# The residual's transposes for the next stage, issued in parts ahead of and between the last products of the sum that completes it, at five places

## What is computed

```
for l in range(2):
    h = rmsnorm(x, g_mix[l]);  z = h @ w_in[l]
    ... short convolution and forgetting attention on z ...
    x = x + concat([y_conv, y_fox]) @ w_out[l]
    hx = rmsnorm(x, g_xa[l])
    x = x + mem_cross_attention(hx, ...) @ w_xo[l]
    hf = rmsnorm(x, g_ffn[l])
    x = x + (swiglu(hf, ...) if l == 0 else moe_swiglu(hf, ...))
```

## Time and profile before

| what | us |
|---|---|
| median of 3 runs | 1334.91 |
| lowest and highest run | 1333.96, 1335.45 |
| span of the profiled execution | 1334.4 |
| PE busy in it | 1313.6 (98%) |
| DVE busy | 1013.7 (76%) |
| ACT busy | 833.1 (62%) |
| POOL busy | 84.6 (6%) |

### The profile page before, as it was taken

One profiled execution on the slowest core, in us unless ns is written; L12 is line 12 of the kernel. 1 busy time (PEld: TensorE's weight loads), 2 busy tenths in 40 slices (PEclk: granted clock), 3 DMA queues, 4 the chain that ended last, 5 costly groups with the idle time before them and its releaser, 6 DMA issues.

```text
span 1334.4 us, 17846 instructions
## 1 busy us (share of the span) xinstructions
PE 1313.6 (98%) x6726; PEld 1122.7 (84%) x6726; DVE 1013.7 (76%) x782; ACT 833.1 (62%) x746; POOL 84.6 (6%) x105
## 2 busy tenths in 40 slices
PE   8999999999999999899999999999999999999998
PEld 6998888888889878788888888888888888888886
DVE  5767764444565776688888888888889888888988
ACT  5545554444455545476767777678677667777674
POOL 4201010000012010200000000000000000000000
PEclk9999999999999999899999999999999999999999
DMA  9633436655597335299999999899999998998994
GB/s 323 195 118 122 151 106 195 200 187 186 181 376 270 122 101 193 66 399 376 341 386 384 346 403 386 347 408 354 374 387 351 399 382 340 417 380 341 413 396 177
DMA packets 117035, 386.18 MB, mean 289 GB/s; under 512 B 6289, under 2 KB 33533, under 8 KB 116989
## 3 DMA queue, kind: packets, MB, share of 16 engines
q1 hardware_dynamic: 105068, 365.08, 73.1%
q0 software_dynamic: 3168, 11.54, 2.2%
q10 hardware_dynamic: 8752, 8.92, 1.9%
HBM read 369.79 MB, written 15.73 MB: 289 GB/s over the span
## 4 chain that ended last, share of the span: by engine, by line
PE 83%; DVE 8%; DMA 3%; ACT 2%; issue 2%; POOL 1%; SPq 0%; DVEq 0%; ACTq 0%
PE bank L1688 34%; PE bank L1684 23%; PE bank L1685 23%; DVE wl L1166 2%; DMA ring<-in_we_gate 2%; DVE wl L1180 2%; PE bank L2264 1%; ACT wh L808 1%; DVE scratch L1324 1%; DVE scratch L1302 1%; DMA ring<-in_we_up 1%; DVE aT_low L1185 1%; PE bank L1877 0%; POOL mfox L693 0%; PE bank L1709 0%
## 5 line engine op out<-in xcount | busy, mean ns | idle before, releaser
L1180 DVE TENSOR_TENSOR wl<-ring,wh 128x2816 fp32r<-128x2816 f32 (+1 forms) x127 | 400.2, 3171 | 58.5 <-PE bank L1688 33.6
L808 ACT ACTIVATE wh<-ring 128x2816 fp32r<-128x2816 f32 (+1 forms) x128 | 336.7, 2632 | 148.1 <-DMA ring<-in_we_gate 43.7
L1166 DVE TENSOR_TENSOR wl<-ring,wh 128x2048 fp32r<-128x2048 f32 (+3 forms) x78 | 185.9, 2383 | 117.0 <-ACT wh L794 116.2
L1684 PE MATMUL bank<-wh,xh 128*128 128x512 f32 (+1 forms) x696 | 264.8, 380 | 4.4 <-DVE wl L1180 3.1
L1685 PE MATMUL bank<-wh,xl 128*128 128x512 f32 (+1 forms) x696 | 263.1, 378 | 0.0
L1688 PE MATMUL bank<-wl,xh 128*128 128x512 f32 (+1 forms) x944 | 241.8, 378 | 0.0
L794 ACT ACTIVATE wh<-ring 128x2048 fp32r<-128x2048 f32 (+3 forms) x77 | 152.8, 1984 | 114.1 <-PE bank L1685 101.2
L1180 DVE TENSOR_TENSOR wl<-ring,wh_third 128x2816 fp32r<-128x2816 f32 (+1 forms) x64 | 187.1, 2923 | 26.7 <-PE bank L1688 23.8
L1688 PEld LDWEIGHTS bank<-wl,xh 128*128 128x128 f32 x944 | 174.8, 188 | 25.4
L808 ACT ACTIVATE wh_third<-ring 128x2816 fp32r<-128x2816 f32 (+1 forms) x64 | 155.5, 2430 | 34.6 <-DMA ring<-in_we_up 16.0
L1684 PEld LDWEIGHTS bank<-wh,xh 128*128 128x128 f32 x696 | 130.6, 188 | 31.2 <-issue 5.6
(11 more groups left out here) (266 smaller groups left out, 1584.2 us busy)
## 6 DMA issues: line engine op xcount, KB each, us to landing
ring<-in_we_gate SPq DMA_DIRECT2D x64, 1408.0 KB, 7.9
ring<-in_we_up SPq DMA_DIRECT2D x64, 1408.0 KB, 8.2
ring<-in_we_down SPq DMA_DIRECT2D x56, 1536.0 KB, 8.8
ring<-in_w_in SPq DMA_DIRECT2D x8, 1536.0 KB, 11.7
ring<-in_w_gate SPq DMA_DIRECT2D x10, 1024.0 KB, 5.1
ring<-in_w_up SPq DMA_DIRECT2D x10, 1024.0 KB, 5.1
ring<-in_w_down SPq DMA_DIRECT2D x10, 1024.0 KB, 4.9
ring<-in_w_in SPq DMA_DIRECT2D x9, 1024.0 KB, 8.6
```

Source lines behind the costliest of these rows:

```text
L808: nc.scalar.activation(wh_in_pass(j, n), ring[:, slot, 0:n], ACT.Copy).then_inc(high_ready, 1)
L1166: nc.vector.tensor_tensor(wl[:, j, 0:n], ring[:, slot, 0:n], wh[:, j, 0:n].bitcast(F32), ALU.subtract).then_inc(low_ready, 1)
L1180: nc.vector.tensor_tensor(wl[:, j % 2, 0:n], ring[:, pass_slot(j), 0:n], wh_in_pass(j, n).bitcast(F32), ALU.subtract).then_inc(low_ready, 1)
L1684: nc.tensor.matmul(dst, x_high, w_high, start=first, stop=False)
```

## The change

`residual_transposed` is cut so that a caller names the row block and the quarters. At five places (`yT` and `zT` of both layers, `xT` of layer 1) the 16 transposes are no longer issued in one run behind the last product. Instead, with the last weight tile: all eight of row block 0 ahead of bank 3's high products; the first four of row block 1 (quarters 0 and 1) between bank 3's high and low products; and the last four (quarters 2 and 3) behind bank 3's low products. The waits of each transpose are as before. `xT` of layer 0, whose residual comes from a transfer, keeps its order. ACT gets one added wait in layer 1: for bank `xw3`, ahead of `gained`.

```diff
                 if l > 0:
+                    act.wait_ge(*full(l, "xw3"))
                     gained(l, "zT", "ffn")
...
-            def residual_transposed(l, names, added):
-                for t in range(TT):
...
+            def residual_transposed(l, names, added, t, quarters):
+                if added is None:
+                    pe.wait_ge(x_loaded[t], 16)
+                for i in quarters:
+                    ps = open_bank(l, f"{names}{i}") if t == 0 else bank(l, f"{names}{i}")
+                    if added is not None and i % 2 == 0:
+                        pe.wait_ge(*taken(0 if added == "d" else l, f"{added}{2 * t + i // 2}"))
+                    for k in range(2):
+                        c = (2 * i + k) * P
+                        ins = nc.tensor.transpose(ps[:, k * S + t * P:k * S + t * P + P], xres[:, t, c:c + P], ident[:])
+                    if t == TT - 1:
+                        ins.then_inc(done(l, f"{names}{i}"), 1)
+
+            def first_rows_transposed(l, names, added):
+                residual_transposed(l, names, added, 0, range(4))
+
+            def second_rows_transposed(l, names, added, half):
+                residual_transposed(l, names, added, 1, (2 * half, 2 * half + 1))
...
-                residual_transposed(l, "xT", None if l == 0 else "d")
+                if l == 0:
+                    first_rows_transposed(l, "xT", None)
+                    second_rows_transposed(l, "xT", None, 0)
+                    second_rows_transposed(l, "xT", None, 1)
+                else:
+                    second_rows_transposed(l, "xT", "d", 1)
...
                         for i in range(4):
                             if last:
+                                if i == 3:
+                                    first_rows_transposed(l, next_input, names)
                                 ins = products(i, False)
                                 if i == 3:
                                     ins.then_inc(highs_used, 1)
+                                    second_rows_transposed(l, next_input, names, 0)
...
-                token_projection("wo", "wo", KT, range(2, 4), {j: taken(l, f"oT{j - 2}") for j in (2, 3)})
-
-
-                residual_transposed(l, "yT", "wo")
+                token_projection("wo", "wo", KT, range(2, 4), {j: taken(l, f"oT{j - 2}") for j in (2, 3)},
+                                 next_input="yT")
+
+
+                second_rows_transposed(l, "yT", "wo", 1)
...
-                residual_transposed(l, "zT", "xw")
+                token_projection("xw", "xo", XH, range(2), {j: taken(l, f"xo{j}") for j in range(2)}, last_heads, "zT")
+
+
+                second_rows_transposed(l, "zT", "xw", 1)
...
                         for q in range(4):
+                            if last and q == 3:
+                                first_rows_transposed(1, "xT", "d")
                             ins = products(q, False)
                             if last:
                                 if q == 3:
                                     ins.then_inc(highs_used, 1)
+                                    second_rows_transposed(1, "xT", "d", 0)
                                 products(q, True).then_inc(done(0, f"d{q}"), 1)
```

More of the change, by code:

```diff
@@ L1991, in heads_transposed, with token_projection @@
                         ins.then_inc(done(l, f"oT{i}"), 1)
-                def token_projection(names, fill, rows, ss, waits, inside=None):
+                def token_projection(names, fill, rows, ss, waits, inside=None, next_input=None):
                     for j in ss:
@@ L2096, in last_heads @@
                     memory_heads(1)
-                token_projection("xw", "xo", XH, range(2), {j: taken(l, f"xo{j}") for j in range(2)}, last_heads)
-                residual_transposed(l, "zT", "xw")
+                token_projection("xw", "xo", XH, range(2), {j: taken(l, f"xo{j}") for j in range(2)}, last_heads, "zT")
+                second_rows_transposed(l, "zT", "xw", 1)
                 if l == 0:
```

## The result

| | us |
|---|---|
| changed kernel, median of 21 runs (lowest to highest) | 1335.36 (1333.23 to 1337.46) |
| kernel before, median of 21 runs on the same chips | 1333.50 (1331.88 to 1335.70) |
| ratio, with its 95% interval | 1.0014 (1.0008 to 1.0020) |
| the same ratio in a second series (11 and 20 runs) | 1.0016 (1.0007 to 1.0025) |
| span of the profiled execution after (before: 1334.4) | 1335.1 |

The change makes the kernel slower by 1.9 us, with an interval of 1.1 to 2.7. I had forecast +3.2 us, 1338.1, with a range from 1335.5. The direction is right, the size is not. The 1335.36 lies just under the range's low end, and that is as much the base as the change: the kernel before has a median of 1333.5 over 21 runs, 1.4 us under the 1334.91 of the three that the prediction started from. With the forecast put on 1333.5, the measured time would still lie 1.3 us under it.

The account below looks back on a forecast made before the run. PE was taken to bound the kernel, busy 1313.6 of 1334.4 us. Delays of 0.8 + 0.8 + 0.33 + 0.4 + 0.9 = 3.2 us on the median 1334.9 gave 1338.1, range 1335.5 to 1340.8.

Parts of the forecast that it names:

- What bounds, and that the place must be late: PE, busy 1313.6 of 1334.4 us, sets the end; at each place the last four transposes wait for the uncovered add.
- The sum: All five places together: 0.8 + 0.8 + 0.33 + 0.4 + 0.9 = 3.2 us slower.
- yT 0.8: yT, each layer: DVE's low parts wait for bank 3 and start later, so the next tile begins 0.8 us later.
- zT 0.33: zT of layer 0: first product 0.46 us later, 0.13 saved by earlier casts, net 0.33 later.
- xT 0.4: xT of layer 1: first product 0.51 us later, 0.12 saved by earlier casts, net 0.4 later.
- logits 0.9: zT of layer 1: the add delays DVE's gain on bank 0, so the logits start 0.9 us later.
- the credit for the early casts: zT of layer 0 and xT of layer 1: first eight products run faster with casts ready, saving 0.13 and 0.12 us.
- 2 for the groups: Rival: moved transpose groups wait for DVE or boundaries cost 0.1 each, adding 1 to 3 us; 1340.1 at middle; chance 0.07.
- Moved transposes and boundaries cost nothing: Twelve transposes per place only end the last products 1.31 us later; no waits; boundaries cost nothing, bound 0 to 1.0 in all.
- partly taken up behind the places: Rival: idle PE time behind the places absorbs delay, leaving 1.9 us at the middle, 1336.8; chance 0.22.
- The rival of the early casts: First products of yT, zT, xT: earlier casts save 4.3 us with logits, against add wait w at five places; chance 0.08.
- The rival of the clock: Routing, 560 to 563 us: moved transposes keep the granted clock high, saving 1.5 us, 1336.6; chance 0.08.

Follow-up runs that it names:

- the two short-add kernels: Changed kernel and kernel before, each with the five last adds covering 1 column instead of 512; first logit -0.04 and +0.03 us against the kernel before.
- after_low_free: Changed kernel, but at yT DVE's input_low no longer waits for the last bank ahead of the first quarter; first logit +1.30 us against the kernel before.
- last_place_old: Changed kernel with the old transpose order at zT of layer 1 alone; first logit +1.80 us against the kernel before, logits 3.71 us.

## Why the prediction was right and wrong

*What bounds, and that the place must be late.* Right. The last add loses its cover, the four transposes behind it wait, and no other stage takes up more than 0.1 of the delay. The idle time of "about 1.2 us" is 1.21 to 1.28, the low parts start 1.5 behind the last product where I had 1.6, and the two short-add kernels show that the add is the cause.

*The sum.* This is the step that failed: 3.2 us of terms where 2.67 stood at the first logit. Term by term, forecast and measured: yT 0.8 and 0.59, zT 0.33 and 0.21, xT 0.4 and 0.30, yT 0.8 and 0.68, logits 0.9 and 0.89. Their errors all point the same way, and come from three places.

At yT the first transpose behind the wait was mis-sized. I took the longest of the line, 0.48, and came to 0.85 from its load to DVE's start; after shows 151.25 to 151.95, 0.70. The 0.48 was no transpose behind such a wait. It stands in the kernel's first microseconds, where every transpose takes 0.42 or more and the clock has not yet risen. The first line is of the kernel before, the second of the changed one:

```profile
L1709 PE MATMUL bank<-ident,xres x16: 421/421/477, 4.8 to 8.1; 128*128 128x128 f32 x16
...
L1709 PE MATMUL bank<-ident,xres x4: 272/272/328, 151.3 to 151.6; 128*128 128x128 f32 x4
```

Behind the wait it took 0.33, and the 0.15 between them is that error: I priced the unknown from the row's maximum without asking where the maximum stands.

At zT and xT the credit for the early casts was mis-sized; the 0.48 is no part of those two terms. I priced the first eight products at 8 x 0.226 = 1.81, so 0.13 and 0.12 saved. Here they are in the changed kernel, at zT of layer 0:

```profile
189.61 1.68 PEld L1689 LDWEIGHTS bank<-wh,xh 128*128 128x128 f32 x8
...
191.34 1.79 PEld L1689 LDWEIGHTS bank<-wl,xh 128*128 128x128 f32 x8
```

They took 191.34 - 189.61 = 1.73, and 1.73 again at xT: 0.21 and 0.20 saved. The other 0.05 at zT are its four transposes, 0.39 from the first load to the next product's where I had 0.44.

A last part at yT: the tile was 0.68 late (0.75 in layer 1), but the stage behind only 0.6 (0.68). Before, DVE's product at 160.18 waited about 0.05 for POOL, which ends at 159.37 + 0.70 = 160.07; after, POOL is not late and DVE's own maximum ends last. The first two lines are of the kernel before:

```profile
159.37 0.70 POOL L724 TENSOR_TENSOR xqr<-xqr,neghalf 128x2 f32<-128x2 f32 x1 [25.66 <-DVEq L1396]
...
160.18 0.16 DVE L1404 TENSOR_TENSOR xnm<-xnm,xqr 128x2 f32<-128x2 f32 x1
...
159.33 0.70 POOL L724 TENSOR_TENSOR xqr<-xqr,neghalf 128x2 f32<-128x2 f32 x1 [25.73 <-DVEq L1397]
159.96 0.69 DVE L1402 TENSOR_REDUCE xnm<-bank 128x2 f32<-128x512 f32 x1 [0.76 <-PE bank L1689]
160.68 0.16 DVE L1405 TENSOR_TENSOR xnm<-xnm,xqr 128x2 f32<-128x2 f32 x1
```

The profile names no releaser for so short a wait before; that it was POOL is worked out from these times (DVE starts 0.09 behind its own maximum's end before, and 0.03 after). I had followed each releaser and said that all had waited for PE. POOL's had not. It accounts for 0.05 of the 0.08 that is taken up; the rest I can't name.

The sum also had no term for the way from the first logit to the first expert product, where 2.6 became 2.3 on the mean of the profiles. What separates that 2.3 from the +1.9 of the medians lies inside the interval. The upper end of the range, 1340.8, is 5.9 over the median, and the terms shown don't give that: 3.2, 1.0 for the boundaries and 2 for the groups make 6.2.

*Moved transposes and boundaries cost nothing.* Right: DVE's last add starts 1.33 us later than before (150.51 against 149.29, and 0.11), against 12 x 0.109 = 1.31, so the two boundaries of that place cost 0.02 together. No first group waited.

*The rival "partly taken up behind the places"* names the very +1.9 at its middle that the time came to, but that is luck: its mechanism is worth 0.08 us at each yT and nothing at zT and xT, where it had half and a third. *The rival of the early casts* was sound as a mechanism and lost on its own condition: the wait w was 1.21, not under 0.86; with the add short, 0.68, the first logit did come out at -0.04 (5w - 4.3 gives -0.9; but yT, where the low parts still wait for the last bank, came to +0.07 and +0.09, and the formula had counted all of its 1.38 as saved). *The rival of the clock* named the right stretch, the routing, and not the cause. The lower level began not behind the logits but inside them, at 552.79 in the profile before, and in nine of the thirteen profiles it began at the same distance from the clock's first rise, wherever the transposes stood. Three executions of the changed kernel have their logits 0.3 us shorter than two before on the mean, which takes 2.67 to about 2.3 at the first expert product; with 3.66 to 6.06 over all executions that can be chance, and it stays open. On the rule of the Trainium skill, "TensorE: Matmul & The Clock Gate", Part 4: PE-mode transpose, that transposes don't count as PE activity: the trace still doesn't show it cost or save anything at these places. The granted clock was 1.00 with the block of 16, and with the block cut up and 1.21 us of idle:

```profile
146.00:157.00 11.00, 9.94 (x66) 8.44 (x65) 7.21 (x16) 7.51 (x14) 0.00 (x0) 1.00 0.30 95
```

*The chances.* I had 0.62 on slower by over 0.2% and 0.30 on within 0.2%; it is 0.14%. The sum of 3.2 lay 0.5 over that line. The two yT terms were priced from one maximum, zT and xT from one pitch, so four of the five erred in two pairs, and all the same way: like terms are one guess, not two.

## What to carry to other kernels

Work that stands between a product and the instruction that needs its result is the cover of that result's way through another engine: before moving it ahead, price the way (here 0.69 for the add and 0.5 for the product's end and the way there and back) and leave that much behind. To start a consumer sooner, first look for an order of the same work that completes the first unit sooner; here that gave 2.0 to 2.1 us up to the first logit, where moving cost 2.7. In the whole time it was 3.5 to 4.0 against 1.9, which is more than the rows up to the logits account for. And where the bound of a stage is a helper that waits for the last unit before it takes the first, what delays the last unit goes to the end of the stage. Before a row's maximum is used as a price, look where in the kernel it stands.

## What the runs showed of the hardware

The granted clock falls from 2.4 to 1.2 GHz in the routing, where PE has only products of eight columns and waits. It falls 2.6 us after the first logit in the first profile before, 3.0 in the first after, 1.0 in after_low_free, and behind all of them in last_place_old. The same 32 products take from 3.66 to 6.06 us by that, and the first expert product moves with them. I had expected the logits to take the same time in every execution.

In nine of thirteen profiles the fall stands 542.7 us behind the clock's first rise, while the first logit stands anywhere from 538.3 to 540.9 behind it: there it doesn't move with the work. In the other four it came earlier or later, and why is open. It isn't that distance alone: with the first logit 538.3 behind the rise in both, the clock fell 1.0 us into the logits in after_low_free and behind them in last_place_old.

At the start of the kernel, before the clock has risen, a transpose of 128x128 takes 421 ns (16 in 3.68 us); behind the rise it takes about 272, and the first behind a wait 328. At the upper level 16 in a row follow each other at 0.109 us.
